# Hybrid HGRN2, Mamba-2 and MoE step: first input and weight transfers cut finer, eight warm-up products, one doubled sum formed once

## Chip, cores and metric

The kernel runs on one core of one Trainium2 chip. The metric is device time of a whole execution in microseconds, the median of three runs. Lower is better.

## What is computed

One layer of a decoder trunk for 256 prompt tokens and 8 x 4 sample tokens, all in float32. Only the start and the sums of `dt * a` matter here:

```python
q, fr, iv, g, z, xbc, dt, gate_a, gate_b = _split_cols(x @ w_in, IN_SPLITS)
...
xbc, conv_new = causal_dwconv(xbc, conv_prev, conv_w, conv_b)
...
acum = jnp.cumsum(dtc * a, axis=1)
...
alast = acum[:, -1]
wdec = jnp.exp(alast[:, None] - acum) * dtc
...
h = layer_norm(ALPHA * x + mix, ln1_g[l], ln1_b[l])
x = layer_norm(ALPHA * h + moe_ffn(h, router_w[l], ...), ln2_g[l], ln2_b[l])
```

`x` is 288 x 1024 with both groups together. `w_in` has 1024 rows. The mixture of experts reads its expert weights in blocks of 64 routed rows, 32 experts, top 4.

## The kernel before

The program is written by hand for the five engines, with semaphores, in blocks that follow each other. The first block projects the columns of `xbc`. TensorE needs `x` transposed (`xT`, 8 row blocks of 128 by 288 tokens), while it is loaded with tokens on partitions (`xtok`, three tiles of 128, 128 and 32 tokens). The weights come in chunks of 512 columns, `ring[0]` and `ring[1]`, 2 MB each. The first chunk is special: it arrives in four transfers of two row blocks, and TensorE works through it row block by row block into four PSUM banks at once, so that it can begin before all of it is there.

In order, TensorE does this (lines 366 to 393). It waits for a tile of ones that POOL writes and runs 12 products of ones by ones whose result is thrown away (the warm-up, L368). Then `turn(0)`, `turn(1)`, `turn(2)`: each transposes one 128-column block of the three token tiles (three records, L377), and VectorE copies the result to `xT` (L318). Then for each row block k from 0 to 7 four products of 128 x 288 (L388; a float32 product has two records in the trace), with `turn(k + 3)` behind the products of k while there is one. `turn` waits for `s_in[0]` before block 0 and for `s_in[1]` before block 4, since x is loaded in two halves of its columns; the products wait for `s_first[0]`, `s_first[1]`, `s_first[2]` and `s_w[0]` before row blocks 0, 2, 4 and 6. Behind this come two transposes of small vectors (L408, L409) and the second chunk (L402).

The transfers are issued from two queues. SyncE (SP) issues, in this order: prompt tile 0 and the sample tile of x's first half, row blocks 0 and 1 of the weights, the three tiles of x's second half, row blocks 2 and 3, 4 and 5, 6 and 7, then `ring[1]`. ScalarE (ACT) issues prompt tile 1 of the first half, waits until x's second half has landed (L277), and then issues the small vectors, the convolution state and the `dt` weights (L278 to L289). After those issues it copies the projection out of PSUM (L293).

After the projection of `xbc` a second block begins, in which the Mamba-2 sums are formed between projection products. `decays(k)` is called behind product k of one such group (L1940) and adds small float32 products: at k = 1, 2, 3 the running sums by token, and at k = 4 and k = 5 twice the same total over both prompt tiles (ones by `d0` plus ones by `d1`, L1926 and L1927), into PSUM columns 96 to 127 and 128 to 159, one for each prompt tile. At k = 6 comes the total of each sample (L1929), into columns 160 to 191. VectorE subtracts the running sums from these totals (L1349).

The last and longest part is the mixture of experts. SP loads the expert weights in pieces of 2 MB into ring places (L816), each time a place is free; TensorE's products read them (L2468, L2473, L2456, L2460).

Of the kernel before, what the change touches and what calls it, by code (L numbers as in the profile page):

```python
# [17 lines left out]
ALU = mybir.AluOpType  # L18
# [3 lines left out]
P = 128  # L22
D = 1024
# [4 lines left out]
KD = D // P  # L28
# [18 lines left out]
C_X = C_Z + INNER  # L47
# [42 lines left out]
def build(nc, x_prompt, x_sample, state_hgrn, state_ssm, state_conv, hg_lower_bounds, w_in, hg_norm_w, hg_proj,  # L90
# [24 lines left out]
    with ctx:  # L115
# [51 lines left out]

        s_in = [S1(f"x_columns_loaded{i}") for i in range(2)]
        s_vec = S1("vectors_loaded")
# [16 lines left out]
        s_ones = S1("ones_ready")  # L186
        s_first = [S1(f"first_chunk_loaded{i}") for i in range(3)]
        s_dtq = S1("dt_quarters_ready")
# [11 lines left out]
        with nc.Block() as block:  # L200
            @block.sync
            def _(sp):
                x_s = x_sample.rearrange("b s d -> (b s) d")
                sp.dma_start(xtok[:, 0, 0:CW], x_prompt[0, 0:P, 0:CW]).then_inc(s_in[0], 16)
                sp.dma_start(xtok[0:32, 2, 0:CW], x_s[:, 0:CW]).then_inc(s_in[0], 16)
                for i in range(4):
                    if i == 1:
                        for t in range(2):
                            sp.dma_start(xtok[:, t, CW:D], x_prompt[0, P * t:P * t + P, CW:D]).then_inc(s_in[1], 16)
                        sp.dma_start(xtok[0:32, 2, CW:D], x_s[:, CW:D]).then_inc(s_in[1], 16)  # L210
                    sp.dma_start(ring[0][:, 2 * i:2 * i + 2, :], w_k[:, 2 * i:2 * i + 2, C_X:C_X + CW]).then_inc(s_first[i] if i < 3 else s_w[0], 16)
                sp.dma_start(ring[1][:], chunk_src(C_X + CW)).then_inc(s_w[1], 16)
                with sp.Fori(1, 3) as i:
                    for n in range(2):

                        sp.wait_ge(s_mt, i * 8 + (4 * n - 4))
                        sp.dma_start(ring[n][:], chunk_src(i * (2 * CW) + (C_X + n * CW))).then_inc(s_w[n], 16)
                for n in range(2):

                    sp.wait_ge(s_mt, CT - 4 + 4 * n)  # L220
                    sp.dma_start(ring[n][:], chunk_src(C_F + n * CW)).then_inc(s_w[n], 16)

                sp.wait_ge(s_nct, 1)
                for j in range(4):
                    sp.dma_start(o_conv_s[0].rearrange("b r (c j m) -> j (b r) c m", j=4, m=32)[j], nrows[32 * j + 3:32 * j + 27, :, :]).then_inc(s_out, 16)
                    sp.dma_start(o_conv_p[0, 0].rearrange("r (c j m) -> j r c m", j=4, m=32)[j], nrows[32 * j:32 * j + 3, :, :]).then_inc(s_out, 16)
                sp.wait_ge(s_out, 128)
# [45 lines left out]
            def _(act):  # L273
                a = nc.scalar
                vr = vrows[0]
                act.dma_start(xtok[:, 1, 0:CW], x_prompt[0, P:2 * P, 0:CW]).then_inc(s_in[0], 16)
                act.wait_ge(s_in[1], 48)  # L277
                act.dma_start(vr[0:96, :], conv_w[0].rearrange("j (c p) -> (j c) p", p=P)).then_inc(s_vec, 16)  # L278
# [85 lines left out]
            def _(pe):  # L364
                m = nc.tensor
                pe.wait_ge(s_ones, 1)
                for _ in range(12):
                    m.matmul(ps[:, 7, 0:P], ones[:], ones[:], start=True, stop=True)  # L368

                def turn(k):  # L370

                    if k >= 4:
                        pe.wait_ge(s_xte, k - 3)
                    if k % 4 == 0:
                        pe.wait_ge(s_in[k // 4], 48)
                    for t, (t0, rows) in enumerate(TILES):
                        last = m.transpose(ps[:, k % 4, t0:t0 + rows], xtok[0:rows, t, k * P:(k + 1) * P], ident[0:rows, 0:rows])  # L377
                    last.then_inc(s_xtp, 1)

                pe.wait_ge(s_ones, 2)  # L380
                for k in range(3):
                    turn(k)
                for k in range(KD):
                    pe.wait_ge(s_xte, k + 1)
                    if k % 2 == 0:
                        pe.wait_ge(s_first[k // 2] if k < 6 else s_w[0], 16)
                    for mt in range(4):
                        last = m.matmul(ps[:, 4 + mt, 0:T], ring[0][:, k, mt * P:(mt + 1) * P], xT[:, k, :],  # L388
                                        start=(k == 0), stop=(k == KD - 1))
                        if k == KD - 1:  # L390
                            last.then_inc(s_mt, 1)
                    if k + 3 < KD:
                        turn(k + 3)

# [351 lines left out]
        with nc.Block() as block:  # L746
# [578 lines left out]
            def _(dve):  # L1325
# [22 lines left out]
                for t, (_, rows) in enumerate(TILES):  # L1348
                    last = v.tensor_tensor(dtmp[0:rows, t, :], ps[0:rows, 4, 96 + 32 * t:128 + 32 * t], av[0:rows, t, :], ALU.subtract)  # L1349
                last.then_inc(q_dif, 1)  # L1350
# [549 lines left out]
            def _(pe):  # L1900
# [13 lines left out]
                def decays(k):  # L1914
# [7 lines left out]
                    if k == 3:  # L1922
                        m.matmul(ps[0:32, 4, 64:96], smask[:], d2, start=True, stop=True)
                    if k in (4, 5):
                        c = 32 * k - 32
                        m.matmul(ps[:, 4, c:c + 32], ones[:], d0, start=True, stop=False)  # L1926
                        m.matmul(ps[:, 4, c:c + 32], ones[:], d1, start=False, stop=True)  # L1927
                    if k == 6:
                        m.matmul(ps[0:32, 4, 160:192], sbatch[:], d2, start=True, stop=True)  # L1929

# [599 lines left out]
```

## Time and profile before

| | us |
|---|---|
| median of 3 runs | 1513.04 |
| lowest, highest run | 1512.48, 1514.04 |
| profiled execution, from its first to its last instruction | 1511.7 |
| TensorE busy in it | 1471.9 |

The profiled execution's own time outside its span is not given; the median of the runs is 1.3 us above the span. In all rows below, time zero is the start of the profiled span. PE is TensorE's products, PEld its weight loads, DVE is VectorE, SPq and ACTq are the queues of SyncE and ScalarE in which transfers are issued.

### The profile page before, as it was taken

Reading aid. Unit: us, or ns where it says so; the run is one execution under the profiler, and the core shown is the slowest. Engines: PE = TensorE matmul, PEld = TensorE weight load, DVE = VectorE, ACT = ScalarE, POOL = GpSimd, SP = SyncE. Lnnn points to the kernel's source line nnn. Section 1 sums busy time; section 2 is a strip of 40 time slices with the busy share of each in tenths; the row PEclk is TensorE's granted clock in tenths of the full one; section 3 lists DMA queues with packets and bytes.
Section 4 is the critical chain, followed back from the end, with each engine's and each line's share of the span. In section 5 each row is a group of like instructions: output and inputs, shape, how many; then the busy total and the mean of one; then the engine's idle time right before and its main releaser. Section 6 shows DMA issues by size and latency. Waiting matters only on the chain.

```text
span 1511.7 us, 22934 instructions
## 1 busy us (share of the span) xinstructions
PE 1471.9 (97%) x9134; PEld 737.1 (49%) x9134; DVE 452.6 (30%) x918; ACT 344.8 (23%) x863; POOL 108.4 (7%) x95
## 2 busy tenths in 40 slices
PE   9999999999999999999999999999999999999997
PEld 7777776556777764333333333333333333333332
DVE  3652788767520136211101101111101101101113
ACT  1224224641210014211212212112112111211213
POOL 1002231010412401000000000000000000000000
PEclk9999999999999999999999999999999999999999
DMA  6346687555269776999999999999999999999996
GB/s 213 112 166 177 197 266 232 195 179 171 96 207 284 301 304 244 427 412 428 429 426 427 427 430 429 428 428 428 430 428 428 427 430 428 429 428 428 430 428 258
DMA packets 110578, 507.81 MB, mean 336 GB/s; under 512 B 12548, under 2 KB 49012, under 8 KB 85844
## 3 DMA queue, kind: packets, MB, share of 16 engines
q1 hardware_dynamic: 103840, 499.64, 82.5%
q10 hardware_dynamic: 6676, 7.29, 1.6%
q8 instruction: 46, 0.75, 0.2%
q14 instruction: 16, 0.13, 0.0%
HBM read 491.19 MB, written 15.72 MB: 335 GB/s over the span
## 4 chain that ended last, share of the span: by engine, by line
PE 63%; DMA 23%; DVE 4%; issue 1%; ACT 0%; DVEq 0%; SPq 0%
DMA wGU<-in_w_gu 23%; PE ps L2468 15%; PE ps L1940 11%; PE ps L2473 7%; PE ps L2236 4%; PE ps L2409 3%; PE ps L1956 3%; PE ps L2456 3%; PE ps L2460 2%; PE ps L2253 2%; PE ps L2266 2%; PE ps L2374 2%; PE ps L2390 1%; PE ps L2020 1%; DVE up L1833 1%
## 5 line engine op out<-in xcount | busy, mean ns | idle before, releaser
L2468 PE MATMUL ps<-wGU,xe 128*64 128x512 f32 x1536 | 343.7, 595 | 15.9 <-DMA wGU<-in_w_gu 15.9
L2473 PE MATMUL ps<-wD,aT 128*64 128x512 f32 x1024 | 226.9, 595 | 0.0
L2468 PEld LDWEIGHTS ps<-wGU,xe 128*64 128x64 f32 x1536 | 108.5, 137 | 238.3 <-issue 211.6
L1940 PE MATMUL ps<-xT,ring 128*128 128x288 f32 (+1 forms) x864 | 181.3, 410 | 1.7 <-PEq L200 0.7
L1829 DVE TENSOR_SCALAR sg<-sg 128x512 f32<-128x512 f32 x32 | 13.7, 427 | 558.6 <-ACT sg L1272 558.6
L1940 PEld LDWEIGHTS ps<-xT,ring 128*128 128x128 f32 (+1 forms) x864 | 124.6, 170 | 46.4 <-issue 3.6
L2473 PEld LDWEIGHTS ps<-wD,aT 128*64 128x64 f32 x1024 | 71.3, 137 | 133.2 <-issue 126.2
L1272 ACT ACTIVATE sg<-ps 128x512 f32<-128x512 f32 x32 | 19.1, 598 | 487.5 <-PE ps L2456 487.5
L1221 ACT ACTIVATE xe<-ps,lnT 128x64 f32<-128x64 f32 x262 | 81.4, 422 | 1.2 <-PE ps L2383 1.2
L402 PE MATMUL ps<-xT,ring 128*128 128x288 f32 x320 | 78.1, 407 | 0.0
L1288 ACT COPY ysb<-ps 64x512 f32<-64x512 f32 x64 | 37.1, 580 | 155.4 <-PE ps L2473 154.6
L402 PEld LDWEIGHTS ps<-xT,ring 128*128 128x128 f32 x320 | 60.6, 190 | 17.1 <-issue 0.5
L2456 PE MATMUL ps<-wGU,xe 128*64 128x512 f32 x256 | 60.8, 595 | 6.4 <-DMA wGU<-in_w_gu 6.4
L2374 PE MATMUL ps<-xres,psel 128*64 128x512 f32 x256 | 65.8, 592 | 0.0
L2236 PE MATMUL ps<-ynT,ringS 128*128 128x288 f32 x256 | 62.2, 406 | 0.0
L2409 PE MATMUL ps<-ysb,gT 128*128 128x512 f32 x128 | 59.7, 607 | 0.7 <-ACT ysb L1288 0.7
L2460 PE MATMUL ps<-wGU,xe 128*64 128x512 f32 x256 | 60.4, 592 | 0.0
L1956 PE MATMUL ps<-ring,xT 128*64 128x512 f32 (+1 forms) x192 | 57.8, 595 | 0.0
L2236 PEld LDWEIGHTS ps<-ynT,ringS 128*128 128x128 f32 x256 | 48.6, 190 | 13.4
L2409 PEld LDWEIGHTS ps<-ysb,gT 128*128 128x128 f32 x128 | 22.8, 189 | 36.1 <-issue 34.3
L1816 DVE TENSOR_TENSOR gsel<-psel,gm 128x192 f32<-128x192 f32 x32 | 11.5, 358 | 87.0 <-PE ps L2473 84.9
L2460 PEld LDWEIGHTS ps<-wGU,xe 128*64 128x64 f32 x256 | 18.4, 137 | 36.6 <-issue 36.6
(487 smaller groups left out, 1437.4 us busy)
## 6 DMA issues: line engine op xcount, KB each, us to landing
wGU<-in_w_gu SPq DMA_DIRECT2D x128, 2048.0 KB, 35.2
wD<-in_w_down SPq DMA_DIRECT2D x64, 2048.0 KB, 36.2
ring<-in_w_in SPq DMA_DIRECT2D x21, 2048.0 KB, 9.1
out<-hst SPq DMA_DIRECT2D x8, 1024.0 KB, 6.0
ringS<-in_ssd_proj SPq DMA_DIRECT2D x4, 2048.0 KB, 8.4
wbuf<-prompt_A_rows ACTq DMA_DIRECT2D x16, 384.0 KB, 3.8
out<-Sb SPq DMA_DIRECT2D x2, 2048.0 KB
ring<-in_hg_proj SPq DMA_DIRECT2D x2, 2048.0 KB, 9.5
```

Source lines behind the costliest of these rows:

```text
L402: last = m.matmul(ps[:, 4 + mt, 0:T], ring[n][:, k, mt * P:(mt + 1) * P], xT[:, k, :], start=(k == 0), stop=(k == KD - 1))
L1221: return a.activation(xe[:, f, h, :], src, ACT.Identity, scale=lnT2[:, f % 2, 2 * h + i:2 * h + i + 1], bias=lnT2[:, f % 2, 4 + 2 * h + i: ...
L1288: a.copy(ysb[h][half, :], ps[BLK * h:BLK * h + BLK, B_Y, :]).then_inc(m_yc, 1)
L1940: last = m.matmul(ps[h, b, 0:T], ring[c % 2][:, k, n * P + h.start:n * P + h.stop], xT[:, k, :], start=(k == 0), stop=(k == KD - 1))
L1956: last = m.matmul(ps[h, b, :], xT[:, k, t0 + h.start:t0 + h.stop], ring[c % 2][:, k, :], start=(k == 0), stop=(k == KD - 1))
L2236: last = m.matmul(ps[:, 7 - c % 2, 0:T], ringS[n % 2][:, k, (c % 2) * P:(c % 2) * P + P], ynT[:, k, :], start=(k == 0), stop=(k == XT_ - 1))
L2374: last = m.matmul(ps[half[h], B_X, :], sel, rows, start=(t == 2), stop=(t == 1))
L2409: return m.matmul(ps[:, ACC[j], :], gT[:, t * P:(t + 1) * P], ysb[j % 2][:], start=False, stop=stop)
L2456: last = m.matmul(ps[half[h], B_G, :], xe[:, 2 + k, 1, :], wgu[n][:, k, CW * h:CW * h + CW], start=False, stop=(k == 1))
L2460: last = m.matmul(ps[half[h], B_U, :], xe[:, 2 + k, 1, :], wgu[n][:, k, D + CW * h:D + CW * h + CW], start=False, stop=(k == 1))
L2468: last = m.matmul(ps[half[h], bank, :], xe[:, f, hx, :], wgu[n][:, k, col + CW * h:col + CW * h + CW], start=(i == 0 and k == 0), stop=False)
L2473: last = m.matmul(ps[half[h], B_Y, :], aT[:, k, i - 4, :], wdn[n][:, k, CW * h:CW * h + CW], start=False, stop=(i == 5 and k == 3))
```

## The change

x is loaded in three parts of its columns: 0 to 255, 256 to 511, 512 to 1023, each with its own semaphore. Row blocks 0 and 1 of the first weight chunk are transfers of their own, issued right behind prompt tile 0 of x's first part. The sample tile of the first part is issued by ACT, and ACT's later transfers wait for the third part. TensorE runs 8 warm-up products and transposes two column blocks ahead of the products, not three. In the second block the total over both prompt tiles is formed once, and VectorE reads it for both.

```diff
-        s_in = [S1(f"x_columns_loaded{i}") for i in range(2)]
+        s_in = [S1(f"x_columns_loaded{i}") for i in range(3)]
...
-                sp.dma_start(xtok[:, 0, 0:CW], x_prompt[0, 0:P, 0:CW]).then_inc(s_in[0], 16)
-                sp.dma_start(xtok[0:32, 2, 0:CW], x_s[:, 0:CW]).then_inc(s_in[0], 16)
-                for i in range(4):
-                    if i == 1:
-                        for t in range(2):
-                            sp.dma_start(xtok[:, t, CW:D], x_prompt[0, P * t:P * t + P, CW:D]).then_inc(s_in[1], 16)
-                        sp.dma_start(xtok[0:32, 2, CW:D], x_s[:, CW:D]).then_inc(s_in[1], 16)
-                    sp.dma_start(ring[0][:, 2 * i:2 * i + 2, :], w_k[:, 2 * i:2 * i + 2, C_X:C_X + CW]).then_inc(s_first[i] if i < 3 else s_w[0], 16)
+                sp.dma_start(xtok[:, 0, 0:256], x_prompt[0, 0:P, 0:256]).then_inc(s_in[0], 16)
+                for k in range(2):
+                    sp.dma_start(ring[0][:, k:k + 1, :], w_k[:, k:k + 1, C_X:C_X + CW]).then_inc(s_first[k], 16)
+                for j, cols in ((1, slice(256, CW)), (2, slice(CW, D))):
+                    for t in range(2):
+                        sp.dma_start(xtok[:, t, cols], x_prompt[0, P * t:P * t + P, cols]).then_inc(s_in[j], 16)
+                    sp.dma_start(xtok[0:32, 2, cols], x_s[:, cols]).then_inc(s_in[j], 16)
+                    sp.dma_start(ring[0][:, 2 * j:2 * j + 2, :], w_k[:, 2 * j:2 * j + 2, C_X:C_X + CW]).then_inc(s_first[1 + j], 16)
+                sp.dma_start(ring[0][:, 6:8, :], w_k[:, 6:8, C_X:C_X + CW]).then_inc(s_w[0], 16)
...
-                act.dma_start(xtok[:, 1, 0:CW], x_prompt[0, P:2 * P, 0:CW]).then_inc(s_in[0], 16)
-                act.wait_ge(s_in[1], 48)
+                act.dma_start(xtok[:, 1, 0:256], x_prompt[0, P:2 * P, 0:256]).then_inc(s_in[0], 16)
+                act.dma_start(xtok[0:32, 2, 0:256], x_sample.rearrange("b s d -> (b s) d")[:, 0:256]).then_inc(s_in[0], 16)
+                act.wait_ge(s_in[2], 48)
...
-                for _ in range(12):
+                for _ in range(8):
                     m.matmul(ps[:, 7, 0:P], ones[:], ones[:], start=True, stop=True)
...
-                    if k % 4 == 0:
-                        pe.wait_ge(s_in[k // 4], 48)
+                    if k in (0, 2, 4):
+                        pe.wait_ge(s_in[k // 2], 48)
...
-                for k in range(3):
+                for k in range(2):
                     turn(k)
                 for k in range(KD):
                     pe.wait_ge(s_xte, k + 1)
-                    if k % 2 == 0:
-                        pe.wait_ge(s_first[k // 2] if k < 6 else s_w[0], 16)
+                    if k < 2 or k % 2 == 0:
+                        pe.wait_ge((s_first[0], s_first[1], s_first[2], None, s_first[3], None, s_w[0])[k], 16)
...
-                    if k + 3 < KD:
-                        turn(k + 3)
+                    if k + 2 < KD:
+                        turn(k + 2)
...
-                    last = v.tensor_tensor(dtmp[0:rows, t, :], ps[0:rows, 4, 96 + 32 * t:128 + 32 * t], av[0:rows, t, :], ALU.subtract)
+                    last = v.tensor_tensor(dtmp[0:rows, t, :], ps[0:rows, 4, 96 + 16 * t:128 + 16 * t] if t != 1 else ps[:, 4, 96:128], av[0:rows, t, :], ALU.subtract)
...
-                    if k in (4, 5):
-                        c = 32 * k - 32
-                        m.matmul(ps[:, 4, c:c + 32], ones[:], d0, start=True, stop=False)
-                        m.matmul(ps[:, 4, c:c + 32], ones[:], d1, start=False, stop=True)
-                    if k == 6:
-                        m.matmul(ps[0:32, 4, 160:192], sbatch[:], d2, start=True, stop=True)
+                    if k == 4:
+                        m.matmul(ps[:, 4, 96:128], ones[:], d0, start=True, stop=False)
+                        m.matmul(ps[:, 4, 96:128], ones[:], d1, start=False, stop=True)
+                    if k == 5:
+                        m.matmul(ps[0:32, 4, 128:160], sbatch[:], d2, start=True, stop=True)
```

The order of TensorE's instructions at the start of the program, before (a row of L377 with 128x32 ends one `turn`; the names in brackets are the semaphores waited for):

```order
L368 MATMUL ps<-ones 128x128 x11
L377 MATMUL ps<-ident,xtok 128x128 [waits x_columns_loaded0,ones_ready]
L377 MATMUL ps<-ident,xtok 128x128
L377 MATMUL ps<-ident,xtok 128x32
L377 MATMUL ps<-ident,xtok 128x128 x2
L377 MATMUL ps<-ident,xtok 128x32
L377 MATMUL ps<-ident,xtok 128x128 x2
L377 MATMUL ps<-ident,xtok 128x32
L388 MATMUL ps<-xT,ring_67 128x288 [waits first_chunk_loaded0,xT_copied]
L388 MATMUL ps<-xT,ring_67 128x288 x3
L377 MATMUL ps<-ident,xtok 128x128 x2
```

and in the change, the same place:

```order
L370 MATMUL ps<-ones 128x128 x7
L379 MATMUL ps<-ident,xtok 128x128 [waits x_columns_loaded0,ones_ready]
L379 MATMUL ps<-ident,xtok 128x128
L379 MATMUL ps<-ident,xtok 128x32
L379 MATMUL ps<-ident,xtok 128x128 x2
L379 MATMUL ps<-ident,xtok 128x32
L390 MATMUL ps<-xT,ring_67 128x288 [waits first_chunk_loaded0,xT_copied]
L390 MATMUL ps<-xT,ring_67 128x288 x3
L379 MATMUL ps<-ident,xtok 128x128 [waits x_columns_loaded1]
L379 MATMUL ps<-ident,xtok 128x128
L379 MATMUL ps<-ident,xtok 128x32
L390 MATMUL ps<-xT,ring_67 128x288 [waits first_chunk_loaded1,xT_copied]
```

Two `turn`s stand ahead of the first product instead of three, and the third has moved behind the first four products, with a wait of its own; the second row block has a wait of its own too.

The order of SP's issues at the start, before:

```order
L204 DMA xtok<-in_x_prompt 128x512
L205 DMA xtok<-in_x_sample 32x512
L211 DMA ring_67<-in_w_in 128x2x512
L209 DMA xtok<-in_x_prompt 128x512 x2
L210 DMA xtok<-in_x_sample 32x512
L211 DMA ring_67<-in_w_in 128x2x512 x3
```

and in the change:

```order
L204 DMA xtok<-in_x_prompt 128x256
L206 DMA ring_67<-in_w_in 128x512 x2
L209 DMA xtok<-in_x_prompt 128x256 x2
L210 DMA xtok<-in_x_sample 32x256
L211 DMA ring_67<-in_w_in 128x2x512
L209 DMA xtok<-in_x_prompt 128x512 x2
L210 DMA xtok<-in_x_sample 32x512
L211 DMA ring_67<-in_w_in 128x2x512
L212 DMA ring_67<-in_w_in 128x2x512
```

The first weights moved from behind two transfers of x to behind one, and x's last part moved from ahead of row blocks 2 and 3 to behind them.

## Rows read from the trace of the kernel before

**Rows 1.** Page of the profile, sections 1 and 2: busy time, and 40 slices.

```profile
PE 1471.9 (97%) x9134; PEld 737.1 (49%) x9134; DVE 452.6 (30%) x918; ACT 344.8 (23%) x863; POOL 108.4 (7%) x95
...
PEclk9999999999999999999999999999999999999999
DMA  6346687555269776999999999999999999999996
```

**Rows 2.** Waits of TensorE, whole span (us in total, times, longest us).

```profile
PE ps L2468 <- DMA wGU<-in_w_gu: 15.9, 24, 1.1
...
PE ps L2030 <- DVE sqa L1538: 1.2, 1, 1.2
```

**Rows 3.** Waits of SP's queue, whole span.

```profile
SPq L816 <- PE ps L2468: 366.2, 93, 7.3
```

**Rows 4.** Stretches (us; PE, PEld, DVE, ACT, POOL busy; PEclk; DMA share; GB/s).

```profile
6.00:8.00 2.00, 2.00 (x11) 1.31 (x10) 0.63 (x2) 0.00 (x0) 1.48 (x9) 1.00 1.01 370
...
560.00:600.00 40.00, 39.66 (x196) 19.95 (x196) 25.06 (x89) 19.28 (x28) 4.86 (x4) 1.00 0.57 215
700.00:1400.00 700.00, 679.59 (x3228) 244.99 (x3226) 92.39 (x253) 136.37 (x337) 0.00 (x0) 1.00 1.01 428
```

**Rows 5.** Timeline of TensorE, first 30 us (start, length, operation, idle time before).

```profile
1.06 5.49 PE L368 MATMUL ps<-ones 128*128 128x128 f32 x24 [1.06 <-POOL ones L233]
...
8.59 2.18 PE L388 MATMUL ps<-xT,ring 128*128 128x288 f32 x8 [0.26 <-DMA ring<-in_w_in]
...
11.09 2.21 PE L388 MATMUL ps<-xT,ring 128*128 128x288 f32 x8
...
21.21 6.09 PE L388 MATMUL ps<-xT,ring 128*128 128x288 f32 x24
27.14 0.27 PE L408 MATMUL ps<-ident,vrows 128*128 128x128 f32 x1
```

**Rows 6.** Timeline of TensorE's weight loads, 5.8 to 9 us.

```profile
6.13 0.44 PEld L377 LDWEIGHTS ps<-ident,xtok 128*128 128x128 f32 x2
6.90 0.48 PEld L377 LDWEIGHTS ps<-ident,xtok 32*128 32x128 f32 x3 [0.33 <-issue]
7.54 0.37 PEld L377 LDWEIGHTS ps<-ident,xtok 32*128 32x128 f32 x3 [0.17 <-issue]
8.09 0.13 PEld L377 LDWEIGHTS ps<-ident,xtok 32*128 32x128 f32 x1 [0.17 <-issue]
```

**Rows 7.** Transfers by source, KB each, us to landing: x in ACT's queue.

```profile
xtok<-in_x_prompt ACTq DMA_DIRECT2D x1, 256.0 KB, 3.2
```

**Rows 8.** Timeline of SP's queue, first 8 us.

```profile
0.81 0.40 SPq L204 DMA_DIRECT2D xtok<-in_x_prompt  x1
1.26 0.41 SPq L205 DMA_DIRECT2D xtok<-in_x_sample  x1
1.73 0.42 SPq L211 DMA_DIRECT2D ring<-in_w_in  x1
```

**Rows 9.** Timeline of VectorE, 7 to 9 us.

```profile
7.25 1.57 DVE L318 COPY xT<-ps 128x288 f32<-128x288 f32 x3 [7.13 <-PE ps L377]
```

**Rows 10.** Landing of the four transfers of L211, each 512 KB.

```profile
DMA to landing us min/median/max: 6.7/8.0/9.2
```

**Rows 11.** Timeline of ACT and its queue, 9 to 25 us.

```profile
10.21 0.35 ACTq L278 DMA_DIRECT2D vrows<-in_conv_w  x1
...
22.55 1.28 ACT L293 ACT_TABLE_LOAD   x1 [22.55 <-issue]
```

**Rows 12.** Timeline of TensorE around the doubled sum, 132 to 134 us.

```profile
132.22 0.73 PE L1940 MATMUL ps<-xT,ring 128*128 128x288 f32 x2
...
132.93 0.39 PE L1927 MATMUL ps<-dta,ones 128*128 128x32 f32 x2
133.16 0.73 PE L1940 MATMUL ps<-xT,ring 128*128 128x288 f32 x2
```

**Rows 13.** Timeline of TensorE, an undisturbed group of L1940.

```profile
123.68 4.12 PE L1940 MATMUL ps<-xT,ring 128*128 128x288 f32 x16 [0.74 <-PEq L200]
```

More of the change, by code:

```diff
@@ L186, in build @@
         s_ones = S1("ones_ready")
-        s_first = [S1(f"first_chunk_loaded{i}") for i in range(3)]
+        s_first = [S1(f"first_chunk_loaded{i}") for i in range(4)]
         s_dtq = S1("dt_quarters_ready")
```

## Prediction

> **What bounds the kernel now.** I read the page first. TensorE is busy for 1471.9 of 1511.7 us, and the DMA engines, at two to seven tenths in most of the first 16 slices, stand at nine from there on [rows 1]. So there are two regimes: up to about 600 us TensorE sets the pace, and after that the expert weights come at full DMA rate. The view of the waits says the same: TensorE waits for nothing longer than 1.2 us at a time, and its largest wait is for the expert weights, 15.9 us in total [rows 2]. In the stretch from 700 to 1400 us the DMA share is 1.01 at 428 GB/s, from 560 to 600 us only 0.57 [rows 4]. The second regime is therefore a stream of fixed length. What this change can do to the end is move the start of the stream, and that start hangs on TensorE: SP issues each piece when a TensorE product has freed a place, in 93 of its waits behind L2468 alone [rows 3], and the stream is not running at full rate before. I take it that a microsecond saved early on TensorE is a microsecond at the end.
>
> The change touches two places: the first 27 us, and about half a microsecond near 132 us. At the front the timeline of TensorE shows no idle time apart from 1.06 us before the first warm-up and 0.26 us before the first product, where the weights landed last [rows 5]. The first transposes start right behind the warm-up, so the first half of x was there by 6.13 us, the first weight load of a transpose [rows 6].
>
> One thing must be read from the lengths. The 24 records of the warm-up start 0.211 us apart ((6.13 - 1.06) / 24) [rows 5, 6], which is 1.65 ns for each of 128 columns. The last 24 product records start 0.247 us apart ((27.14 - 21.21) / 24), 0.86 ns for each of 288 columns [rows 5]. So the warm-up ran at the lower of the two clock levels, 1.2 GHz, though the clock line prints full speed for the slice [rows 1]. The rise fell into the transposes: their third weight loads are 0.64 and then 0.55 us apart, and the first group needed 0.77 us from its first load to its third [rows 6]. I put the rise at about 7.2 us.
>
> **The change, part by part.** I work out when L408 starts, which is at 27.14 us now [rows 5].
>
> Warm-up: 4 products fewer are 8 records by 0.211 us. The warm-up ends 1.69 us earlier and the first transpose's weights load at 6.13 - 1.69 = 4.44 us, if x is there. x's first part is 128 + 128 + 32 KB, half of what it was. ACT's 256 KB landed 3.2 us after their issue at about 0.8 us, so at 4.0 us [rows 7, 8]. Half as many bytes should be there no later, 4.0 to 4.4 us with the second issue of ACT; I cost this wait at nothing. Its bound from above is the 6.13 us of now.
>
> First product: it stands behind two groups of transposes. At the lower clock a group costs at most twice its 0.55 us; the first group shows 0.77 us from first to third load, and with the next step of about 0.24 us some 1.0 us. So TensorE is through both at 4.44 + 2.0 = 6.45 us. The copy of block 0 is no later: now it starts 7.25 - 6.13 = 1.12 us after the first load and the three take 1.57 us [rows 6, 9], so it is done by 4.44 + 1.12 + about 0.5 = 6.1 us. The weights of row block 0 are now 256 KB, second in SP's queue (1.26 us), where 512 KB were third (1.73 us) and landed 6.7 us later, at 8.43 us [rows 8, 10]. Ahead of that landing stood 1088 KB; ahead of the new one, itself included, stand 544 KB. With x's 4.0 us as the least and 8.43 us as the most, I take half of the way by bytes, about 5.2 to 5.5 us. No wait, so the first product starts at 6.45 us instead of 8.59 us, 2.14 us earlier.
>
> From there to L408: now it takes 27.14 - 8.59 = 18.55 us, with five groups of transposes among the products. One more moves in. A row block with a group takes 2.50 us (11.09 - 8.59) to 2.53 us, a row block alone 5.93 / 3 = 1.98 us [rows 5], so the moved group costs 0.55 to 0.59 us here. That makes 19.14 us. This cost is no new work; it is the third group that stood ahead before.
>
> Clock: between 6.45 and 7.2 us the products now run at half speed, where before transposes stood; that costs half of the stretch, 0.4 us. So L408 starts at 6.45 + 19.14 + 0.4 = 26.0 us, 1.1 us earlier.
>
> The later waits of the block: x's second part has 1088 KB ahead of its landing (itself included), the same as the first weights before, so 8.43 us; it is wanted behind the first row block's products, at about 6.45 + 1.98 + 0.4 = 8.8 us. Tight, no cost, at worst some tenths. Row block 1 is ahead of it in the queue. Blocks 2 and 3 and x's third part come later in bytes by at most 512 KB but are wanted 2.5 us and more apart, and the transfers ran at 370 GB/s from 6 us on [rows 4]; 512 KB take 1.4 us, so the DMA has room. I cost them at nothing; if the cover fails, the bound is the last landing in this queue now, 9.2 us after its issue [rows 10].
>
> ACT's queue: its small transfers now wait for x's third part, behind which 512 KB more have gone by; that is 512 KB at 370 GB/s, 1.4 us [rows 4]. They begin at 11.6 us instead of 10.21, and ACT is free for its copies at 23.83 + 1.4 = 25.2 us (its table load ends at 22.55 + 1.28) [rows 11]. The first product bank is ready near 24.7 us; the copy is needed only when TensorE comes back to that bank, behind L408. The new lateness of ACT is thus about as large as the cover. Nothing to some tenths of a microsecond; I take nothing. TensorE's own lead over ACT then grows again with every bank (four banks of 2 us each against copies of about 0.6 us).
>
> Doubled sum: a projection pair with the two products of ones behind it takes 133.16 - 132.22 = 0.94 us [rows 12]; an undisturbed pair takes 4.12 / 8 = 0.515 us [rows 13]. One of two such insertions goes, 0.43 us. The sample total only moves from k = 6 to k = 5. VectorE does the same three subtractions from other columns. This is in TensorE's regime, so it counts in full.
>
> Sum: 1.1 + 0.43 = 1.55 us. Against the profiled execution, 1511.7 - 1.55 = 1510.1 us of span; the median of the runs stands 1.3 us above that span, so **1511.5 us**.
>
> **The rivals.** First, **the clock rises later** (the case on the other side). With a third of the warm-up gone, and two groups of short transposes directly behind it, TensorE does less before the point at which the clock rose. Every microsecond that it rises later costs half a microsecond of products. The gain of 1.55 us is used up when it rises 3.1 us later, at 10.3 us, and beyond it the kernel is slower: at 12 us, 1513.9 us. It would need a rise at about 16.4 us to be slower by 0.2%. For it speaks that the first group's loads have idle gaps of 0.33 and 0.17 us, and that the rise came so late, 6 us after the first record; against it, that transposes filled the last microsecond before the rise and did not prevent it [rows 6]. The Trainium skill, page "TensorE: Matmul & The Clock Gate", section "Part 4: PE-mode transpose", says that transposes do not count as TensorE being busy in the way products do; that rule would make this rival the likely one, since the change puts the transposes where four warm-up products were. I give the late rise 30%: two thirds of that ends between 1511.9 and 1513.3 us, one third above.
>
> Second, **the finer transfers land no earlier**. If rows of 1 KB and the fixed part of a transfer's time eat what the halving saves, and row block 0 lands at 8.43 us as before, the first product starts at 8.59 us and L408 at 27.73 us, 0.59 us later than now; with the doubled sum 1513.2 us. The 3.2 us for 256 KB against 6.7 us behind 1088 KB speak for a landing that follows the bytes [rows 7, 10]. 10%.
>
> Third, **the gain is lost on the way**: ACT becomes late, or the weights' stream does not start earlier. Then 1512.6 to 1513.0 us. SP's waits on TensorE speak against it [rows 3]. 8%.
>
> Fourth, more gain: the clock rises early in this kernel's executions, already in the warm-up, so that the transposes are short and no product is slow. The first product at 5.9 us, L408 at 25.1 us: 2.0 us, with 0.43 us 2.5 us, 1510.6 us. 7%. The forecast keeps 45%.
>
> **How the numbers follow.** A measurement of this kernel can tell about 0.2% from no change, 3.0 us. None of the cases reaches that on either side by its own sum; the runs of before alone spread over 1.6 us. Faster by over 0.2%: 5%, for a term that I do not see. Slower by over 0.2%: 3%, for a clock that stays low for ten microseconds. Within 0.2%: 92%. The predicted time is that of the likeliest case. The range takes in the more-gain case with the spread of a median below (1510.2) and the late-clock and late-transfer cases above, up to a rise at about 11.5 us (1513.7).
>
> **What would show it.** In the profile of the changed kernel: the first transposes at about 4.6 us and the first product near 6.5 us, with no DMA wait before it; product records of double length up to some point, which dates the clock's rise; the vector transpose near 26.0 us; one pair of insertions between the projection products near 131 us instead of two; and the stretch of the expert weights at the same 428 GB/s, about 1.6 us earlier. A first product behind a wait for `ring` would show the second rival, long product records past 10 us the first. The forecast is wrong if the front saves more than 2.5 us or loses time.

## The result, and the profile after

The change makes the kernel slower: 1516.97 us median of 20 runs (1514.38 to 1519.52) against 1512.93 us median of 20 runs of the kernel before (1511.00 to 1514.41). The ratio is 1.0025, with a 95% interval from 1.0019 to 1.0031. The forecast was 1511.5 us, within a range that ended at 1513.7 us. One slow run stands among the 33 of the kernel before that were taken beside e5 to e8 (2532.26 us, mean clock 0.556); the intervals use fast runs alone.

The page of the changed kernel hides the reason almost wholly. Its clock line is the same as in [rows 1], its DMA line differs by a tenth in two of 40 slices, and TensorE has 12 records fewer.

```profile
span 1513.6 us, 22915 instructions
...
PE 1470.0 (97%) x9122; PEld 735.0 (49%) x9122; DVE 452.5 (30%) x918; ACT 345.0 (23%) x863; POOL 108.4 (7%) x95
...
DMA  6346677555369776999999999999999999999996
...
q8 instruction: 46, 0.75, 0.2%
```

The profiled execution took 1515.33 us, span 1513.6 us, so 1.7 us lie around the span.

The timeline of TensorE at the start, which answers to [rows 5]:

```profile
1.06 3.78 PE L370 MATMUL ps<-ones 128*128 128x128 f32 x16 [1.06 <-POOL ones L234]
4.63 1.26 PE L379 MATMUL ps<-ident,xtok 128*128 128x128 f32 x6
5.89 2.21 PE L390 MATMUL ps<-xT,ring 128*128 128x288 f32 x8
7.94 0.56 PE L379 MATMUL ps<-ident,xtok 128*128 128x128 f32 x3
8.43 2.21 PE L390 MATMUL ps<-xT,ring 128*128 128x288 f32 x8
...
25.06 0.27 PE L410 MATMUL ps<-ident,vrows 128*128 128x128 f32 x1
```

There is no DMA wait in it. The first product starts at 5.89 us where it started at 8.59, and the small transposes behind the block at 25.06 us where they started at 27.14: between these two executions the front saves 2.08 us, more than the 1.1 us forecast. The start varies from one execution to the next, though: with the old start unchanged, the profiles of e1 and e11 below reach L408's transpose at 26.57 and 26.52 us. Against those the new front saves 1.5 us. Near 130 us the doubled sum is gone as well: one pair of products of ones is left, and the sample total follows one projection pair later.

```profile
129.19 0.75 PE L1941 MATMUL ps<-xT,ring 128*128 128x288 f32 x2
129.78 0.30 PE L1927 MATMUL ps<-dta,ones 128*128 128x32 f32 x2
129.92 0.39 PE L1928 MATMUL ps<-dta,ones 128*128 128x32 f32 x2
130.14 0.73 PE L1941 MATMUL ps<-xT,ring 128*128 128x288 f32 x2
130.81 0.24 PE L1930 MATMUL ps<-dta,sbatch 32*32 32x32 f32 x2
130.98 1.24 PE L1941 MATMUL ps<-xT,ring 128*128 128x288 f32 x4
```

I laid the two TensorE timelines over each other, record by record. Behind the sum the changed kernel is 2.52 us ahead. It stays so until about 200 us. Then it falls behind, and this is where. First the kernel before, 200 to 214 us:

```profile
203.38 1.17 PE L2007 MATMUL ps<-bm,xw 32*128 32x128 f32 x32
204.48 4.15 PE L1940 MATMUL ps<-xT,ring 128*128 128x288 f32 x16
208.56 1.90 PE L2020 MATMUL ps<-hT,cT 32*32 32x128 f32 x128
```

and the changed one (lines are one higher):

```profile
200.86 0.72 PE L2008 MATMUL ps<-bm,xw 32*128 32x128 f32 x15
201.92 0.73 PE L2008 MATMUL ps<-bm,xw 32*128 32x128 f32 x17 [0.35 <-issue]
...
206.66 1.47 PE L2021 MATMUL ps<-hT,cT 32*32 32x128 f32 x95
210.84 0.58 PE L2021 MATMUL ps<-hT,cT 32*32 32x128 f32 x33 [2.71 <-issue]
```

These are groups of short products of the state read-out and the state update, written one behind the other with no semaphore between them. The group of 128 records stops after 95, for 2.71 us, and the group of 32 after 15, for 0.35 us. The releaser is "issue": TensorE waited for nothing that the profile shows. With both pauses and what follows them, the lead of 2.5 us has become a lag of 1.0 us at that place (211.35 against 210.39 us for the next group); a longer wait for VectorE at L2031 (1.8 us, before 1.2 us [rows 2]) takes it to 1.7 us, and the span ends 1.9 us late. The expert stretch is unchanged: 679.59 us busy between 700 and 1400 us and 428 GB/s, as in [rows 4].

So the question is why a pause without a semaphore appears 180 us behind the new start and 75 us behind the new sum, in code that was not edited.

### The profile page after: what moved, and what is told of

The parts are those of the page before. It is cut to its first block, busy times and chain, and to the rows that moved or that the text cites. A ratio compares the mean times of both kernels' runs of the same rounds, so it can differ in the third digit from the quotient of the medians.

```text
span 1513.6 us, 22915 instructions
## 1 busy us (share of the span) xinstructions
PE 1470.0 (97%) x9122; PEld 735.0 (49%) x9122; DVE 452.5 (30%) x918; ACT 345.0 (23%) x863; POOL 108.4 (7%) x95
## 4 chain that ended last, share of the span: by engine, by line
PE 65%; DMA 22%; DVE 4%; issue 1%; ACT 0%; DVEq 0%; SPq 0%
DMA wGU<-in_w_gu 21%; PE ps L2469 16%; PE ps L1941 11%; PE ps L2474 8%; PE ps L2237 4%; PE ps L2410 3%; PE ps L1957 3%; PE ps L2457 3%; PE ps L2461 3%; PE ps L2254 2%; PE ps L2375 2%; PE ps L2267 1%; PE ps L2391 1%; DVE up L1835 1%; DVE up L1834 1%
```

## The experiments

**Two theories.** Theory 1: TensorE's instructions are loaded in blocks, and the removed products shift the block borders within the program; a border that falls into a run of short products, while the DMA engines are full, leaves TensorE without instructions. The trace's code packets are visible: 46 of them, 0.75 MB, 16 KB each. The Trainium skill, page "Advanced Engine Details and Errata", section "ISA Cache", gives cache lines of 16 KB, which are 256 instructions. The packet size here agrees, and so does the distance of 254 to 256 records between two stops, found under e4. The same section of the Trainium skill says that there are only two lines, but also gives TensorE 128 KB; no run here shows which of the two holds. Theory 2: the work at the front comes earlier, or is issued in another way, and collides with transfers. All experiments were timed beside fresh runs of the kernel before, in three groups, each on another chip: e1 to e4 (its median 1512.71 us, 25 runs), e5 to e8 (1512.84 us, 33 runs) and e9 to e12 (1512.75 us, 33 runs). The ratio is that of the record, with its 95% interval in brackets; it is not the quotient of the two medians, and can differ from it by 0.0007. The experiments have 11 runs each, e2 nine and e4 five. Where a profile is read, it is of one execution.

**e1: the sum alone.** The kernel before with this edit:

```diff
...
-                    if k in (4, 5):
-                        c = 32 * k - 32
-                        m.matmul(ps[:, 4, c:c + 32], ones[:], d0, start=True, stop=False)
-                        m.matmul(ps[:, 4, c:c + 32], ones[:], d1, start=False, stop=True)
+                    if k == 4:
+                        m.matmul(ps[:, 4, 96:128], ones[:], d0, start=True, stop=False)
+                        m.matmul(ps[:, 4, 96:128], ones[:], d1, start=False, stop=True)
...
```

> Only the doubled sum is formed once; the start of the program is as before. Two products fewer on TensorE. Theory 1 (code position: TensorE's code arrives in blocks, and a block's border that falls into a run of short products while the DMA engines are full makes TensorE pause): 0.4 us faster by the sum, plus whatever pause the shift of two products brings, so anything from 0.4 us faster to 4 us slower, with a pause marked 'issue' inside L2021's group if it is slower. Theory 2 (the earlier start makes transfers collide): 0.4 us faster, 1512.5 us, no pause.

1513.66 us, before 1512.71: slower, if anything, by 0.09% (1.0000 to 1.0018). A removal of two products, 0.4 us of work, did not pay. The group of 32 pauses after 8 records for 0.55 us, the group of 128 after 87 for 0.38 us:

```profile
203.43 0.95 PE L2006 MATMUL ps<-bm,xw 32*128 32x128 f32 x24 [0.55 <-issue]
208.39 1.41 PE L2019 MATMUL ps<-hT,cT 32*32 32x128 f32 x87
210.17 0.87 PE L2019 MATMUL ps<-hT,cT 32*32 32x128 f32 x41 [0.38 <-issue]
```

**e2: the front alone.** The change with the sum doubled as before:

```diff
...
+                    if k in (4, 5):
+                        c = 32 * k - 32
+                        m.matmul(ps[:, 4, c:c + 32], ones[:], d0, start=True, stop=False)
+                        m.matmul(ps[:, 4, c:c + 32], ones[:], d1, start=False, stop=True)
...
```

> The new start (three parts of x, row blocks alone, 8 warm-up products), the sum doubled as before. Theory 1: the front saves 2.1 us; four products fewer ahead of L2021's group move the code borders, so it ends between 2 us faster and 4 us slower. Theory 2: the loss belongs to the earlier start, so it is as slow as the change or a little more, 1517 us.

1516.47 us, ratio 1.0032 (1.0022 to 1.0042): as slow as the whole change. By itself this fits both theories. The pause is there, after 91 records, and the group of 32 stops after 11 for 0.45 us.

```profile
202.25 0.94 PE L2009 MATMUL ps<-bm,xw 32*128 32x128 f32 x21 [0.45 <-issue]
...
207.20 1.44 PE L2022 MATMUL ps<-hT,cT 32*32 32x128 f32 x91
211.07 0.84 PE L2022 MATMUL ps<-hT,cT 32*32 32x128 f32 x37 [2.44 <-issue]
```

**e3: the change, padded.** Products of 32 x 1 put the old numbers back:

```diff
                 for _ in range(8):
                     m.matmul(ps[:, 7, 0:P], ones[:], ones[:], start=True, stop=True)
+                for _ in range(4):
+                    m.matmul(ps[0:32, 7, 0:1], ones[:, 0:32], ones[:, 0:1], start=True, stop=True)
...
+                    if k == 6:
+                        for _ in range(2):
+                            m.matmul(ps[0:32, 4, 160:161], ones[:, 0:32], d0[:, 0:1], start=True, stop=True)
```

> The change, with four warm-up products of 32 x 1 and, at k = 6 behind the projection product, two of 32 x 1 added, so that every later TensorE instruction has the same number in the program as before. Some 0.3 us of extra work. Theory 1: the pauses go back to where they were, and the kernel is 1.8 to 2.3 us faster than before, about 1511.0 us, with no pause inside L2021's group near 208 us. Theory 2: as slow as the change, about 4 us above before.

1512.11 us, ratio 1.0002 (0.9993 to 1.0011): it takes back nearly all of the change's loss, by adding work. The pause is gone in its profile, whose span is 1510.3 us:

```profile
207.06 1.90 PE L2026 MATMUL ps<-hT,cT 32*32 32x128 f32 x128
```

But the median falls short of the 1511.0 that theory 1 expected: the 11 runs lie between 1510.76 and 1515.20 us, four of them above 1514. More on that below.

**e4: the kernel before with 8 wide warm-up products.** TensorE has the same 1536 warm-up columns, and four products fewer; no transfer is changed.

```diff
-                for _ in range(12):
-                    m.matmul(ps[:, 7, 0:P], ones[:], ones[:], start=True, stop=True)
+                for _ in range(8):
+                    m.matmul(ps[:, 7, 0:192], ones[:], ones[:, 0:1].broadcast_to([P, 192]), start=True, stop=True)
```

> The kernel before, its 12 warm-up products of 128 columns replaced by 8 of 192 columns: the same time on TensorE, four products fewer in the code, nothing else changed. Theory 1: slower by 1 to 5 us, with a pause inside a group of short products. Theory 2: no difference within 0.5 us.

1517.28 us, ratio 1.0035 (1.0021 to 1.0048), in five runs. No transfer was changed and no useful work, and the loss is as large as that of the change. Theory 2 does not quite fall here: in this profile, too, the start came earlier, the first product at 7.29 us and L408 at 25.83 us, 1.31 us ahead of [rows 5]. It falls by comparison with e3 and e5, whose profiles are as early or earlier (25.62 and 25.00 us at the same transpose) and have no such pause, while e1's, at 26.57 us, has. The timeline of TensorE in e4:

```profile
7.29 2.18 PE L388 MATMUL ps<-xT,ring 128*128 128x288 f32 x8 [0.28 <-DMA ring<-in_w_in]
...
203.23 0.94 PE L2007 MATMUL ps<-bm,xw 32*128 32x128 f32 x20 [0.44 <-issue]
204.10 4.15 PE L1940 MATMUL ps<-xT,ring 128*128 128x288 f32 x16
208.18 1.44 PE L2020 MATMUL ps<-hT,cT 32*32 32x128 f32 x91
212.05 1.06 PE L2020 MATMUL ps<-hT,cT 32*32 32x128 f32 x37 [2.44 <-issue]
213.04 5.57 PE L1940 MATMUL ps<-xT,ring 128*128 128x288 f32 x16
```

Three readings. First, the record behind which the pause stands: with 2, 4, 4 and 6 products removed (e1, e2, e4, the change) it is 87, 91, 91 and 95, two records for each product, since a float32 product has two. e2 and e4 have different transfers and different warm-up products, share the number of products, and stop behind the same record. The pause is tied to a position counted from the start of the program, as a block border is. Second, the distance between the two stops is the same in all five profiles that have both: in e1 24 + 16 + 87 = 127 product records, in e2 128, in e4 127, in the change and in e6 128. With one weight load for each that is 254 to 256 records, a fixed distance, as between the borders of equal blocks. Third, the products behind the pause are slow, 5.57 us for 16 records instead of 4.15. The stretches show why (us, PE busy, PEclk, DMA share, GB/s):

```profile
208.00:212.00 4.00, 1.61 (x93) 1.00 1.11 316
212.60:215.90 3.30, 3.30 (x11) 0.50 0.95 295
216.00:220.00 4.00, 4.00 (x45) 1.00 0.10 27
```

Behind a stretch in which TensorE was busy for 1.61 of 4 us, the granted clock was at its lower level, 1.2 GHz, for some 3.4 us. The group of 16 records shows 1.42 us of its cost, and by half of 3.4 us it would be 1.7 us in all, an estimate. The profiles of e2, e4 and e6 show this fall, that of the change does not; but 12 of its 20 runs have a mean clock of 0.996 or 0.997, and their median is 2.4 us above that of the eight runs with 0.998 or 0.999 (1517.68 against 1515.31 us). So some of the runs may well have had the fall that the profiled one lacks, which would explain why the profile (1515.33) shows less than the median (1516.97); their clocks' course is not on record.

**e5 and e6: where the six small products stand.** In e5 at the end of the first block, 85 us ahead of the pause; in e6 right behind it.

```diff
                     last.then_inc(s_mt, 1)
+                for _ in range(6):
+                    m.matmul(ps[0:32, 0, 0:1], ones[:, 0:32], ones[:, 0:1], start=True, stop=True)
```

> The change with six products of 32 x 1 added at the end of the first block, about 85 us ahead of the pause, beside TensorE's wait for the block's end. The start and the sum are the change's own. Theory 1 (code position): the pause near 208 us is gone, 2 to 2.5 us faster than before, about 1510.6 us. Rival (the pause belongs to the new start or the new sum as such, for example to transfers that come 2.5 us earlier): as slow as the change, 1516 to 1517 us.

> The same six small products, but behind the place of the pause, right before the head pairs. Theory 1: nothing ahead of the pause has changed against the change, so the pause stays, 1516 to 1518 us. Rival (it is the total number of products or the length of the program that matters): as fast as with the six ahead.

e5: 1512.05 us, ratio 0.9996 (0.9987 to 1.0005). e6: 1516.25 us, 1.0022 (1.0013 to 1.0031). The same six products, 4.2 us apart by their place alone. e6 stops behind record 95, exactly as the change, and e5 nowhere. First e6, then e5:

```profile
211.25 0.84 PE L2021 MATMUL ps<-hT,cT 32*32 32x128 f32 x33 [2.62 <-issue]
```

```profile
200.88 1.17 PE L2010 MATMUL ps<-bm,xw 32*128 32x128 f32 x32
...
206.06 1.91 PE L2023 MATMUL ps<-hT,cT 32*32 32x128 f32 x128
```

e5's profiled execution is the fastest profiled one of the study, 1509.57 us, with a span of 1507.8 us. Its lead over the kernel before is still 2.5 us at 215 us and 2.3 us at 900 us: front and sum are kept when nothing stops TensorE. Another 1.6 us come between 900 and 1500 us, in the expert stretch, where nothing was changed; such differences, to either side, stand in other profiles too. In the median of 11 runs e5 is only 0.8 us below the kernel before, which its interval does not tell from no change, and it misses the 1510.6 us expected.

**e7: less data beside the pause.** The change, with 64 KB of each sample state stored where it was 1 MB; the rest of that output is left out.

```diff
-                    sp.dma_start(rows_of(o_ssm_s, b), hst[b % 4][:]).then_inc(q_h[b % 4], 16)
+                    sp.dma_start(rows_of(o_ssm_s, b)[:, 0:1, :], hst[b % 4][:, 0:1, :]).then_inc(q_h[b % 4], 16)
```

> The change, but of each sample state 64 KB are stored in the second block where it was 1 MB (the rest of that output is left out). The DMA engines are then much less full between 150 and 240 us. If the code block comes late because it queues behind the data: the pause inside L2021's group falls under 1 us and the kernel ends 2 to 5 us earlier than the change. If it comes late because TensorE's sequencer asks for it late, the pause stays at more than 2 us.

1513.58 us, ratio 1.0006 (0.9997 to 1.0015), 3.4 us less than the change. Not all of that is the pause: nothing tells what the smaller stores save in the kernel before, which was not tried, and in the profiles e7 is 1.9 us ahead of the change at 900 us and 3.0 us at 1500. The code is the same, and so is the place of the stop, but its length is not:

```profile
207.04 1.47 PE L2021 MATMUL ps<-hT,cT 32*32 32x128 f32 x95
209.13 0.58 PE L2021 MATMUL ps<-hT,cT 32*32 32x128 f32 x33 [0.61 <-issue]
```

2.71 us have become 0.61; another stop, of 0.65 us, shows in the same kind of group at 186 us, where the change has none. So the length of the pause depends on what the DMA engines carry. It is not the only part: between 200 and 240 us the kernel before has a DMA share of 0.83 and no stop, the change 0.78 and the stop.

**When the code arrives.** In the DMA view of narrow stretches, the code packet ahead of the group of 32 starts between 196.5 and 199 us in the kernel before, in a stretch in which the data take 54.1% of the engines:

```profile
q1 hardware_dynamic: 716, 0.37, 54.1%
q8 instruction: 1, 0.02, 2.9%
```

In the changed kernel, which is 2.5 us ahead, the same stretch has no code packet; it comes between 199 and 201 us, beside data that fill the engines:

```profile
q1 hardware_dynamic: 466, 0.68, 98.7%
q8 instruction: 1, 0.02, 2.9%
```

The next one comes between 208 and 210 us, when the group of 128 is already under way (it began at 206.66). In the kernel before it came between 205 and 208 us, ahead of the group's start at 208.56. In the change:

```profile
q8 instruction: 1, 0.02, 3.6%
```

The trace ties the stops to these packets. In the change the two packets ran from 199.55 to 200.48 us and from 208.29 to 209.44 us, and TensorE went on at 201.92 and 210.84 us, 1.4 us behind the end of each. It is so for all 16 stops marked "issue" that the 14 profiles have between 30 and 300 us, short and long, with much or little data beside them: each ends 1.3 to 1.5 us behind the end of a code packet. That is theory 1 seen directly: TensorE stands until its next block of code is there.

Why the packet starts so late is not shown. The change is 2.5 us ahead, and its packets start 2.4 and 1.8 us later. One reading is that the border slipped from ahead of some wait of TensorE's to behind it, and with that the request for the next block; no run tested it.

**e8, e12: fourteen small products.** The change with `range(14)` in place of e5's `range(6)`, run twice.

> The change with fourteen small products at the end of the first block, eight more than restore the old positions. Theory 1: the code borders lie eight products earlier than in the kernel before, on the other side from the change; the pause may be gone for good (1510.8 us, with a smaller spread than with six) or stand at another group. The rival says as slow as the change.

> e8 again, as the version that may beat both: front, sum once and fourteen small products. 1 to 2 us faster than before, 1511 to 1511.8 us; where the pause inside L2021's group is absent in the profile, TensorE's first product at about 6 us.

1511.59 and 1511.51 us; ratios 0.9990 (0.9981 to 0.9999) and 0.9995 (0.9986 to 1.0004). It is the best version by the median, about 0.1% below the kernel before, and only the first of the two measurements separates them. It missed the 1510.8 us expected of e8. No pause stands inside L2021's group, but both profiles have a shorter one a little later, of 0.56 us at 220.75 us in e8 and of 0.24 us at 222.50 us in e12. The spread is no smaller than that of e5: 1509.44 to 1515.40 us in e12. The profile of e12 shows one reason. It reads at the start:

```profile
4.67 1.76 PE L379 MATMUL ps<-ident,xtok 128*128 128x128 f32 x6
6.36 3.99 PE L390 MATMUL ps<-xT,ring 128*128 128x288 f32 x8
10.18 0.56 PE L379 MATMUL ps<-ident,xtok 128*128 128x128 f32 x3
```

The first eight product records take 3.99 us, not 2.21: the clock was still at its lower level, until about 10 us. In the changed kernel's profile it had risen by 5 us.

**e9 and e10: which part of the front pays.** e9 is the change with 12 warm-up products and two small ones at the end of the first block; e10 is the kernel before with 8 warm-up products and four small ones there.

```diff
-                for _ in range(8):
+                for _ in range(12):
...
```

> The change with all 12 warm-up products (finer transfers, two blocks transposed ahead, sum once) and two small products at the end of the first block, so that all later products stand where they stood before. If the front's gain comes from ending the warm-up earlier: the first product starts at about 7.7 us instead of 8.59, minus the transposes that move behind it, so the front gives only 0.3 us and the kernel 0.7 us (1512.1 us). If it comes from the finer transfers alone: as e5, 2 us or more.

> The kernel before with 8 warm-up products and its old transfers, and four small products at the end of the first block, so that the later positions are as before. The first product still waits for the first 512 KB of weights, until 8.4 us: 0.2 us faster at most, within noise of before, with a DMA wait of 1 to 2 us ahead of L388. If the warm-up were the whole gain, 1.5 us faster.

e9: 1511.99 us, ratio 0.9992 (0.9983 to 1.0001), 11 runs between 1511.25 and 1513.99 us. Its first product starts at 7.39 us and L410 at 26.56 us, 0.58 us earlier than before. e10: 1513.76 us, ratio 1.0000 (0.9991 to 1.0009). The timeline and the stretches of e10:

```profile
5.15 1.67 PE L377 MATMUL ps<-ident,xtok 128*128 128x128 f32 x9 [0.31 <-DMA xtok<-in_x_sample]
8.29 3.86 PE L388 MATMUL ps<-xT,ring 128*128 128x288 f32 x8 [1.48 <-DMA ring<-in_w_in]
```

```profile
8.40:11.80 3.40, 3.40 (x8) 0.50 1.05 383
```

With the old transfers TensorE waits 1.48 us for the weights, and the clock, already high, fell to 0.50 until 11.8 us. So in these profiles neither part gives the gain alone: the finer transfers make room, the shorter warm-up uses it. The medians do not bear it out or refute it: the intervals of e5, e9 and e10 overlap.

**e11: the kernel before with e8's positions.** The eight small products are added at the end of its first block.

> The kernel before with eight small products at the end of the first block: the code positions of e8, nothing else. If these positions are better than those of before by themselves, 0.5 us or more faster; if they only avoid the pause, the same as before within 0.5 us.

1513.13 us, ratio 1.0002 (0.9993 to 1.0011). The positions of e8 are not better than those of before; both only avoid the long pause. What e8 gains, if it gains, it gains at the front and by the sum.

Over all 14 profiles: with products removed ahead of L2020's group (the change, e1, e2, e4, e6, e7) it is interrupted in six of six; with the old number (the kernel before, e3, e5, e9, e10) or eight more (e8, e11, e12) in none of eight. The start of these profiles, dated by the transpose at L408, lies anywhere from 24.85 to 28.53 us and does not sort them.

## Why the prediction was wrong

- **The step that failed** is the last sentence of the first paragraph: a microsecond saved early on TensorE is a microsecond at the end. Where no stop stands in the way it held in the profiles (e5's lead is 2.5 us at 150 us and 2.3 us at 900 us). What the working left out is that removing instructions is not only time saved. I counted the edit in time alone, and costed the removal of six products at their own duration. In code they are also six products fewer ahead of everything else, and by e4 four fewer cost 4.6 us by the medians (1517.28 against 1512.71). In the change the two stops took 3.5 us out of a lead of 2.5 us, and a longer wait for VectorE 0.7 us more.
- **The front** came out better than forecast, 2.08 instead of 1.1 us, and just as my fourth rival (7%) had it: the first product at 5.89 us for 5.9, the transpose at 25.06 us for 25.1. The warm-up term was right (1.69 us; the transposes' first records start 6.34 - 4.63 = 1.71 us earlier). The clock was the mis-sized term: I took it to rise at 7.2 us as in the one profile I had, which made both transposes and the first product slow; here both groups took 1.26 us, and the first eight product records took their full-speed 2.21 us. The size of the gain is partly luck: executions of the same start differ, and the old start's first product came at 8.59, 8.02 and 7.97 us (before, e1, e11), so some 0.6 of the 2.08 us is a late execution of the kernel before.
- **The transfers** came earlier than worked out by bytes (5.2 to 5.5 us for row block 0): the two row blocks landed 3.2 and 3.7 us after their issues at 1.26 and 1.7 us, so by 4.5 and 5.4 us, and no wait stood before the first product. The second rival did not happen.
- **The sum** gave 0.44 us, as forecast: the lead over the kernel before grows from 2.08 us at 121.6 us to 2.52 us behind the sums (the first product behind them at 134.67 us, in the change at 132.15).
- **ACT** was not late: its table load began at 21.64 us, earlier than before [rows 11], since its transfers of the state took 6.35 us and not 7.92. I had worked this out as a narrow cover; it was never tested.
- **The first rival**, a late clock, is real but belongs to other executions: the profile of e12 shows it, at 10 us, at a price of about 2 us at the front, and e10 shows a fall for a wait of 1.48 us. The profile of the change does not show it at the start. There it rose at 4.94 us, 0.3 us into the transposes, and in e6 at 6.21 us, 1.6 us into them; in e12 it stayed low through them. The Trainium skill's rule (page "TensorE: Matmul & The Clock Gate", section "Part 4: PE-mode transpose"), that transposes do not count as TensorE being busy in the way products do, would have made the late rise the likely case; of the nine profiles with the new front one has it, and the runs decide no more than that. In e2, e4 and e6 the clock fell behind the pause. My rival had the right price per microsecond at the wrong place.
- **The third rival** named ACT and the start of the weights' stream as the places where the gain could be lost. It was lost on TensorE itself, in a pause with no semaphore. Its price was capped at the gain, and so was my range; a pause that adds its own time and the clock's has no such cap.
- **The 1.3 us** between span and median: in every later run the time is 1.7 or 1.8 us above its own span. By that the profiled execution of before took some 0.5 us more than the median one (an estimate), about as much as its start was late. The forecast is not touched, since it comes to the median less the gain; the leads named here against that profile are.
- The chance of 3% for slower by over 0.2% was too small. The profile of before held a sign that I did not use: the page lists 46 code packets, and in the trace they are spread over the span up to 794 us, so code is loaded while TensorE runs.

## What to carry to other kernels

A long, unrolled instruction stream such as this one is loaded while it runs, so adding or removing instructions moves every later border between blocks of code. When a local saving is there in the timeline and the total is not, lay the two timelines over each other, look for idle time marked "issue" inside a run of identical short instructions, and count the record it stands behind; then pad with a few tiny instructions ahead of it, and once behind it as a control. And read the spread with the median. A single profile can be 1.5 us off in a part that was not changed, as the expert stretch shows here. With 11 runs each, the versions with 12 warm-up products spread over 2.7 to 2.9 us (e1, e9, e11), those with 8 of the same width over 4.0 to 6.0 us (e3, e5 to e8, e10, e12), with old transfers as with new. The kernel before, with 12, spreads over 3.4 us in 20 runs and 6.2 us in 33, so this is a sign and no proof.

## What the runs showed of the hardware

- Two float32 products removed move a stop by four records, 87 to 91 to 95, 75 to 200 us later; four products fewer, with the same warm-up columns, cost 4.6 us of 1512.7 (e4).
- A stop ends 1.3 to 1.5 us behind the end of a 16 KB code packet, in 16 of 16 cases; two neighbouring stops are 127 or 128 product records apart, with as many weight loads.
- Stops of 2.44 to 2.62 us in the middle of short products took the granted clock from 1.00 to 0.50 for 3.4 us (e2, e4, e6), one of 2.71 us in the change did not; a wait of 1.48 us behind transposes did so too (e10), while in e11 one of 1.00 us did not.
- The same stop was 2.71 us beside DMA engines at a share of 0.78 (200 to 240 us) and 0.61 us beside 0.52 (e7).
- Open: whether a wait of TensorE's holds back the request for the next block, and which; and what the spread from run to run is made of. The shorter warm-up goes with a wider one, and a late clock (e12) or a fall at the first wait (e10) would account for some of it, but only the profiled executions show their clock's course. Some arises elsewhere: between 900 and 1500 us, in unchanged code, the 13 other profiles gain up to 1.6 us on that of the kernel before (e5) or lose up to 1.0 us (e8, e9).
